# The first two modulation vectors of a diffusion trunk step: three pairs of split buffers, and the token norm and turns spread over both vectors

## Chip, cores and metric

The kernel runs on one core of a Trainium2 chip, as one launch. The metric is the time of an execution on the device in microseconds (us). A profile covers one execution.

## What is computed

The reference is one inference step of a one-layer trunk: 512 latent and 128 context tokens, 2048 channels. The part around the change is the first modulation and norm, which the value projection needs (`c` for the latent, `c_ctx` for the context tokens):

```python
m = silu(cvec) @ w_mod + b_mod                 # (2048) @ (2048 x 12288), for c and for c_ctx
sh1, sc1, g1, sh2, sc2, g2 = split(m, 6)
h = rmsnorm(x, g_pre1) * (1 + sc1) + sh1       # 640 tokens x 2048
proj = h @ w_in                                # value columns are made first
```

Then come a bidirectional recurrence and differential attention, their projections, and a mixture of 16 experts. All weights are float32.

## The kernel before

**Splitting.** Every float32 weight is cut into a high and a low part for TensorE: ScalarE copies the tile in `raw` (four slots of 128 x 2048, 1 MiB each) into `w_hi` (L339), VectorE subtracts it from the tile into `w_lo` (L348). `w_hi` and `w_lo` have two slots each (NHL). SP loads a tile as two DMAs of 512 KB (`load`, L432 to L436) once the low part of the tile four earlier is made. ScalarE makes a high part only when TensorE is done with the tile two earlier (`halves_used`). With `fine=True` all this goes by halves of 1024 columns.

**First two vectors.** Shift and scale (sh1, sc1) are columns 0 to 4095 of w_mod, 16 tiles of 128 x 2048 for each vector, group g = 0 and g = 1, taken in the order of the k rows. TensorE multiplies each tile by a 128 x 4 stationary `c_hl` (silu(c) and silu(c_ctx), high and low), eight matmuls of 512 columns a tile (L385, L386, in `by_halves`). Group 0 accumulates in banks 4 to 7 of PSUM, group 1 in banks 0 to 3. At a group's end VectorE and ScalarE each copy half of the row (`mod_half`, L1165 and L808), TensorE turns it into columns (`turn_rows`), and VectorE adds the bias and makes the scale (`mod_columns`, L1149 to L1154).

**Tokens.** ScalarE's queue issues the five token blocks of 1 MiB (128 tokens x 2048) behind tiles 5, 7, 9, 11 and 13 of group 0. In group 1, every third tile, ScalarE squares a block (`square`, L775, with its root, L777), VectorE makes a diagonal of the reciprocals (`norm_diagonal`, L1133, L1135), TensorE turns and scales the block by 16 matmuls against that diagonal into banks 4 to 7 (`turn_x`, L1739), and ScalarE and VectorE take two banks each into `xT` (`take_x`, L783 and L1140). Once the second row is in columns, `tokens(k)` makes h in its high part (ScalarE) and its low part (VectorE, L1159), and the value projection starts (`wide`, matmuls on L419 to L421): two halves of 512 columns, each of four tiles of w_in. The five blocks of a half are copied into `v_stage` by VectorE (`take_values`, L1194).

**Small loads and POOL.** ScalarE's queue first issues c, c_ctx, the gain g_pre1, the bias and the identity; TensorE waits for all five (80) and turns the 80 rows (L1727), VectorE copies the columns (L1124), ScalarE applies Silu (L763). In program order ScalarE makes the high part of tile 0 before that. POOL issues 11 parameter loads (L588), sets `zero` and writes it over the 5 MiB accumulator `d_f` of the experts in five DMAs (L594) that wait for nothing else. Then, for each value half, it stores `v_stage` (L600, L602) and waits for the store, which frees `v_stage`. The parameters are turned by TensorE behind everything else of this stage.

**Order.** Each engine's order is written out by hand; the engines meet only at semaphores. The rest of the kernel (input projection with modulation vectors 2 to 5 made on VectorE, heads, output, experts) is untouched.

Of the kernel before, what the change touches and what calls it, by code (L numbers as in the profile page):

```python
# [22 lines left out]
P = 128  # L23
# [34 lines left out]
N_PAR = 11  # L58
# [5 lines left out]
MOD_FROM = [sum(MOD_TILES[:n]) for n in range(8)]  # L64

# [37 lines left out]
def trunk(nc, a, out_ctx, out_lat, out_k, out_v, out_state):  # L103
    ctx = ExitStack()
    with ctx:
# [42 lines left out]
        def place(at0, items):  # L148

            o, made = at0, {}  # L150
            for name, shape, dt in items:
# [10 lines left out]
                       ("zero", [P, D], F32), ("rows1", [80, P], F32), ("rows2", [105, P], F32),  # L162
                       ("cols1", [P, 80], F32), ("cols2", [P, 105], F32),
# [4 lines left out]
        A["diag"] = at("diag", [P, 2, P], F32, s0 + 50048 + 256)  # L168
        c_hl = at("c_hl", [P, KT, 4], F32R, s0 + 50048)
# [7 lines left out]
        assert s0 + 15360 + 2 * UB <= PLACED["rows1"] and PLACED["ones2"] + 64 <= s0 + 50048  # L177
# [90 lines left out]
        par_loaded, x_lat_loaded, x_ctx_loaded = sem("par_loaded"), sem("x_lat_loaded"), sem("x_ctx_loaded")  # L268
# [34 lines left out]
        LATER = {"state_turned": ("rows_turned", 2), "state_row": ("cols_ready", 2), "state_stored": ("c_loaded", 80),  # L303
# [75 lines left out]
        def by_halves(pe, u, slot, out, c, start, stop):  # L379

            for p in range(2):
                pe.wait_ge(lo_ready, 2 * NRAW + 2 * u + p + 1)
                for n in (2 * p, 2 * p + 1):
                    s = slice(n * 512, (n + 1) * 512)
                    pe.matmul(out[:, n, :], c, w_lo[:, slot, s], start=start, stop=False)  # L385
                    last = pe.matmul(out[:, n, :], c, w_hi[:, slot, s], start=False, stop=stop)  # L386
                last.then_inc(halves_used, 1)
# [170 lines left out]
        def _(pool):  # L558
# [14 lines left out]
            def heads(x):  # L573
# [10 lines left out]
                     (r2[104:105, :], a["g_sub"])]  # L584
            loads += [(A["lamv"][0:1, i, :], a[n]) for i, n in enumerate(("lam_q1", "lam_q2", "lam_k1", "lam_k2"))]
# [165 lines left out]
        def _(act):  # L751
# [11 lines left out]
            act.activation(A["sc"][:], A["cols1"][:, 0:32], ACT.Silu).then_inc(S["c_act"], 1)  # L763
# [31 lines left out]
            for k in range(KT):  # L795
                split_hi(act, Q_MOD, k + 1, fine=True)
                if k >= 4 and k % 2 == 0 and (k - 4) // 2 < TT:
                    t = (k - 4) // 2
                    if t < TT - 1:
                        act.dma_start(x_in[:, t, :], a["x_sample"][0][t * P:(t + 1) * P, :]).then_inc(x_lat_loaded, 16)  # L800
                    else:
                        act.dma_start(x_in[:, t, :], a["x_prompt"][0]).then_inc(x_ctx_loaded, 16)

            def mod_half(g):

                act.wait_ge(halves_used, used((Q_MOD + g * 4 + 4) * 4))
                b = 6 - 4 * g
                act.activation(A[f"m_row{g}"][:, 1024:2048].rearrange("p (b n) -> p b n", b=2), ps[0:4, b:b + 2, :], ACT.Copy  # L808
                               ).then_inc(S["row_act"], 1)

            for k in range(KT):
                split_hi(act, Q_MOD + 4, k + 1, fine=True)
                if k == 0:
                    mod_half(0)
                if k % 3 == 0 and k < 3 * TT:
                    square(k // 3)
                if k % 3 == 0 and k:
                    take_x(k // 3 - 1)
# [290 lines left out]
        def _(dve):  # L1109
# [14 lines left out]
            dve.tensor_copy(A["cols1"][:], ps[:, 7, 0:80]).then_inc(S["cols_ready"], 1)  # L1124
# [3 lines left out]
            split_lo(dve, Q_MOD, 0)  # L1128
# [14 lines left out]
            def mod_columns(g, h):  # L1143
# [5 lines left out]
                own.done(TTn(dst, r[:, 0:2, :], A["cols1"][:, None, 48 + n:56 + n].to_broadcast([P, 2, 8]), ALU.add))  # L1149
                own.settle()  # L1150
                own.done(TTn(dst, r[:, 2:4, :], dst, ALU.add))
                if g:
                    own.settle()
                    STT(A["A1"][:, :, 8 * h:8 * h + 8], dst, 1.0, A["cols1"][:, None, 32 + 8 * h:40 + 8 * h].to_broadcast([P, 2, 8]),  # L1154
# [6 lines left out]
            def mod_half(g):  # L1161

                dve.wait_ge(halves_used, used((Q_MOD + g * 4 + 4) * 4) - 1)
                b = 4 - 4 * g
                dve.tensor_copy(A[f"m_row{g}"][:, 0:1024].rearrange("p (b n) -> p b n", b=2), ps[0:4, b:b + 2, :]  # L1165
                                ).then_inc(S["m_row_ready"], 1)

            for k in range(KT):
                split_lo(dve, Q_MOD, k + 1, fine=True)
            for k in range(KT):  # L1170
                split_lo(dve, Q_MOD + 4, k + 1, fine=True)
                if k == 0:
                    mod_half(0)
                if k == 1:
                    mod_columns(0, 0)
                    mod_columns(0, 1)
                if k % 3 == 1 and k < 3 * TT:
                    norm_diagonal(k // 3)
                if k % 3 == 0 and k:
                    take_x(k // 3 - 1)  # L1180
# [19 lines left out]
            dve.wait_ge(S["rows_turned"], 2)  # L1200
            dve.tensor_copy(A["cols2"][:], ps[:, 5, 0:105]).then_inc(S["cols_ready"], 1)

            dve.wait_ge(S["cols_ready"], 2)
# [519 lines left out]
        def _(pe):  # L1723
# [5 lines left out]
            pe.wait_ge(S["c_loaded"], 80)  # L1729
            turn(ps[:, 7, 0:80], A["rows1"][:], 80).then_inc(S["rows_turned"], 1)  # L1730
# [12 lines left out]
            def mod_group(g, after=()):  # L1743

                b = 4 - 4 * g
                for k in range(KT):
                    by_halves(pe, Q_MOD * NRAW + g * KT + k, k % 2, ps[0:4, b:b + 4, :], c_hl[:, k, :], k == 0, k == KT - 1)
                    if k in after:
                        after[k]()

            def turn_rows(g):

                if g:
                    pe.wait_ge(S["xt_act"], 2 * TT)
# [9 lines left out]
            def turn_parameters():  # L1764
                pe.wait_ge(par_loaded, N_PAR * 16)
                pe.wait_ge(S["xt_dve"], 2 * TT)
# [8 lines left out]
            mod_group(0)  # L1775
            turns = {3 * t + 2: (lambda t=t: turn_x(t)) for t in range(TT)}
# [344 lines left out]
```

## Time and profile before

| | us |
|---|---|
| median of 3 runs (lowest, highest) | 3057.34 (3056.35, 3059.58) |
| the profiled execution's own time | 3056.34 |
| its span, from first to last instruction | 3054.8 |
| TensorE matmuls busy | 2882.4 (94%) |
| VectorE, ScalarE, GpSimd (POOL) busy | 2141.5, 1544.1, 289.8 |

The mean granted TensorE clock is 0.973 of full speed (2.4 GHz). All places on the time axis count from the span's start. "Busy" of TensorE takes in overlapping, pipelined matmuls. A chain of waits is followed back from the last instruction: at each step to what released it. A table of windows gives each engine's busy time in a stretch, the granted clock (PEclk), the mean busy share of the 16 DMA engines and their GB/s. In timelines and groups, x and a number counts instructions, and the bracket says what the engine waited for.

### The profile page before, as it was taken

Reading aid. Unit: us, or ns where it says so; the run is one execution under the profiler, and the core shown is the slowest. Engines: PE = TensorE matmul, PEld = TensorE weight load, DVE = VectorE, ACT = ScalarE, POOL = GpSimd, SP = SyncE. Lnnn points to the kernel's source line nnn. Section 1 sums busy time; section 2 is a strip of 40 time slices with the busy share of each in tenths; the row PEclk is TensorE's granted clock in tenths of the full one; section 3 lists DMA queues with packets and bytes.
Section 4 is the critical chain, followed back from the end, with each engine's and each line's share of the span. In section 5 each row is a group of like instructions: output and inputs, shape, how many; then the busy total and the mean of one; then the engine's idle time right before and its main releaser. Section 6 shows DMA issues by size and latency. Waiting matters only on the chain.

```text
span 3054.8 us, 42269 instructions
## 1 busy us (share of the span) xinstructions
PE 2882.4 (94%) x15607; PEld 2304.1 (75%) x15607; DVE 2141.5 (70%) x1836; ACT 1544.1 (51%) x1469; POOL 289.8 (9%) x349
## 2 busy tenths in 40 slices
PE   5899999999999999989999995999999999999993
PEld 1589999998788888879997774666666666666662
DVE  4737797795566666653344457888888888888886
ACT  4931212213455555542233343777777777777773
POOL 1000000002111111100000000011000000111100
PEclk8999999999999999999999997999999999999997
DMA  9737686683333333344433564899999999999995
GB/s 387 275 92 261 206 273 220 207 286 114 116 115 115 115 115 115 115 150 126 121 111 137 196 231 174 347 372 389 379 389 378 395 386 382 387 379 381 381 393 218
DMA packets 292998, 758.17 MB, mean 248 GB/s; under 512 B 20328, under 2 KB 184736, under 8 KB 228144
## 3 DMA queue, kind: packets, MB, share of 16 engines
q1 hardware_dynamic: 266768, 638.80, 57.5%
q0 software_dynamic: 23680, 102.59, 10.3%
q10 hardware_dynamic: 2480, 15.84, 1.3%
q8 instruction: 44, 0.72, 0.1%
q14 instruction: 26, 0.21, 0.0%
HBM read 700.94 MB, written 56.22 MB: 248 GB/s over the span
## 4 chain that ended last, share of the span: by engine, by line
PE 81%; DVE 9%; DMA 5%; issue 3%; ACT 2%; DVEq 0%; POOL 0%; SPq 0%; POOLq 0%; ACTq 0%
PE ps L419 15%; PE ps L420 14%; PE ps L421 14%; PE ps L1814 8%; PE ps L1816 7%; PE ps L1815 7%; DVE mod_acc L1261 4%; PE ps L1948 2%; PE ps L1950 2%; PE ps L1949 2%; PE ps L1727 2%; DMA raw<-in_w_mod 2%; DVE w_lo L348 1%; PE ps L1877 1%; PE ps L1899 1%
## 5 line engine op out<-in xcount | busy, mean ns | idle before, releaser
L373 DVE TENSOR_TENSOR we_lo<-raw,we_hi 128x2048 fp32r<-128x2048 f32 x384 | 876.4, 2290 | 138.9 <-ACT we_hi L368 137.9
L368 ACT ACTIVATE we_hi<-raw 128x2048 fp32r<-128x2048 f32 x384 | 736.5, 1919 | 287.6 <-PE ps L421 287.6
L1814 PE MATMUL ps<-hi,w_lo 128*128 128x320 f32 x2048 | 647.2, 316 | 9.4 <-DVE w_lo L348 5.1
L1816 PE MATMUL ps<-hi,w_hi 128*128 128x320 f32 x2048 | 634.2, 310 | 0.0
L1815 PE MATMUL ps<-lo,w_hi 128*128 128x320 f32 x2048 | 634.0, 310 | 0.0
L348 DVE TENSOR_TENSOR w_lo<-raw,w_hi 128x2048 fp32r<-128x2048 f32 (+1 forms) x184 | 349.8, 1918 | 254.9 <-ACT w_hi L339 248.7
L339 ACT ACTIVATE w_hi<-raw 128x2048 fp32r<-128x2048 f32 (+1 forms) x184 | 292.5, 1610 | 281.5 <-PE ps L421 156.2
L1814 PEld LDWEIGHTS ps<-hi,w_lo 128*128 128x128 f32 x2048 | 385.8, 188 | 28.2 <-issue 14.9
L419 PE MATMUL ps<-we_hi,xs_lo 128*80 128x512 f32 x1024 | 402.2, 393 | 2.2 <-DVE xs_lo L1658 2.2
L420 PE MATMUL ps<-we_lo,xs_hi 128*80 128x512 f32 x1024 | 402.7, 393 | 0.0
L421 PE MATMUL ps<-we_hi,xs_hi 128*80 128x512 f32 x1024 | 400.1, 391 | 0.0
L1815 PEld LDWEIGHTS ps<-lo,w_hi 128*128 128x128 f32 x2048 | 385.9, 188 | 1.4
L1816 PEld LDWEIGHTS ps<-hi,w_hi 128*128 128x128 f32 x2048 | 385.5, 188 | 0.0
L1261 DVE SCALAR_TENSOR_TENSOR mod_acc<-mod_raw,sc,mod_acc 128x2048 f32<-128x2048 f32 x120 | 276.7, 2347 | 3.6
L419 PEld LDWEIGHTS ps<-we_hi,xs_lo 128*80 128x80 f32 x1024 | 151.6, 148 | 87.2 <-issue 2.8
L421 PEld LDWEIGHTS ps<-we_hi,xs_hi 128*80 128x80 f32 x1024 | 151.6, 148 | 84.2 <-issue 0.5
L420 PEld LDWEIGHTS ps<-we_lo,xs_hi 128*80 128x80 f32 x1024 | 151.7, 148 | 82.3 <-issue 0.4
L419 PE MATMUL ps<-we_hi,hid_lo 128*80 128x512 f32 x512 | 202.3, 395 | 0.5 <-DVE hid_lo L1678 0.4
L421 PE MATMUL ps<-we_hi,hid_hi 128*80 128x512 f32 x512 | 200.7, 392 | 0.0
L420 PE MATMUL ps<-we_lo,hid_hi 128*80 128x512 f32 x512 | 200.5, 392 | 0.0
L1948 PE MATMUL ps<-hi,w_lo 128*128 128x320 f32 x512 | 160.9, 314 | 14.7 <-DVE lo L1448 9.6
L1949 PE MATMUL ps<-lo,w_hi 128*128 128x320 f32 x512 | 159.6, 312 | 0.0
(339 smaller groups left out, 3704.5 us busy)
## 6 DMA issues: line engine op xcount, KB each, us to landing
raw<-in_w_e_gate SPq DMA_DIRECT2D x128, 1024.0 KB, 7.2
raw<-in_w_e_up SPq DMA_DIRECT2D x128, 1024.0 KB, 6.9
raw<-in_w_e_down SPq DMA_DIRECT2D x128, 1024.0 KB, 12.0
raw<-in_w_in SPq DMA_DIRECT2D x144, 512.0 KB, 5.1
mod_raw<-in_w_mod SPq DMA_DIRECT2D x64, 1024.0 KB, 5.1
raw<-in_w_mod SPq DMA_DIRECT2D x64, 512.0 KB, 7.7
raw<-in_w_o SPq DMA_DIRECT2D x64, 512.0 KB, 4.7
d_proj<-stage POOLq DMA_DIRECT2D x32, 320.0 KB, 3.3
```

The lines of the kernel that those rows point to most:

```text
L339: act.activation(w_hi[:, j % NHL, s], raw[:, j, s], ACT.Copy).then_inc(hi_ready, 1 if fine else 2)
L348: dve.tensor_tensor(w_lo[:, j % NHL, s], raw[:, j, s], w_hi[:, j % NHL, s].bitcast(F32), ALU.subtract).then_inc(lo_ready, 1 if fine else 2)
L368: act.activation(we_hi[:, k % NEH, :], raw_slot(k), ACT.Copy).then_inc(hi_ready, 2)
L373: TTn(we_lo[:, k % NEH, :], raw_slot(k), we_hi[:, k % NEH, :].bitcast(F32), ALU.subtract).then_inc(lo_ready, 2)
L419: pe.matmul(out, s_lo, m_hi, start=start, stop=False)
L420: pe.matmul(out, s_hi, m_lo, start=False, stop=False)
L421: return pe.matmul(out, s_hi, m_hi, start=False, stop=stop)
L1261: last = STT(mod_acc[:, v, :], w, c, mod_acc[:, v, :], ALU.mult, ALU.add)
L1814: pe.matmul(out, wl, hi[:, k, ms], start=(k % 16 == 0), stop=False)
L1815: pe.matmul(out, wh, lo[:, k, ms], start=False, stop=False)
L1816: last = pe.matmul(out, wh, hi[:, k, ms], start=False, stop=(k == KT - 1))
L1948: pe.matmul(out, wl, hi[:, k, ms], start=(k % 8 == 0), stop=False)
```

## The change

A third pair of buffers, `w3_hi` and `w3_lo`, is laid over space that `mod_raw` takes later; tile m of the 32 (both groups in one count) uses pair m mod 3, so ScalarE waits for TensorE to be done with the tile three earlier. Both groups accumulate in banks 0 to 3, and tile 16 waits until the first row has been copied out. Token loads, squares, turns and takes are spread over all 32 tiles. The gain g_pre1 and the bias leave ScalarE's first loads for POOL's parameter loads (`rows3`), and are turned, with the other parameters, behind tile 3 of TensorE. Silu is applied once to a constant ahead of the data. Tile 0's high part now stands behind c's on ScalarE. POOL writes the zeros only after the first value half, ahead of its store. `cols1` shrinks to c and c_ctx, and the values of LATER go with it.

```diff
-N_PAR = 11
+N_PAR = 13
+X_LOAD = (1, 4, 8, 13, 17)
+X_SQUARE = (6, 11, 16, 22, 26)
+X_DIAG = (7, 12, 17, 23, 27)
+X_TAKE = (10, 15, 20, 26, 30)
...
+        w3_hi, w3_lo = at("w3_hi", [P, D], F32R, mod_at), at("w3_lo", [P, D], F32R, mod_at + UB)
+        c_hl = at("c_hl", [P, KT, 4], F32R, mod_at + 2 * UB)
+        A["diag"] = at("diag", [P, 2, P], F32, mod_at + 2 * UB + 256)
...
+        def mod_w(m):
+            return ((w_hi[:, 0, :], w_lo[:, 0, :]), (w_hi[:, 1, :], w_lo[:, 1, :]), (w3_hi[:], w3_lo[:]))[m % 3]
+        def tile_hi(act, m):
+            act.wait_ge(raw_loaded[m % NRAW], (m // NRAW + 1) * INC)
+            for p in range(2):
+                if 2 * m + p > 1:
+                    act.wait_ge(halves_used, 2 * m + p - 1)
+                act.activation(mod_w(m)[0][:, half_of(p)], raw[:, m % NRAW, half_of(p)], ACT.Copy).then_inc(hi_ready, 1)
+        def tile_lo(dve, m):
+            for p in range(2):
+                dve.wait_ge(hi_ready, 2 * m + p + 1)
+                dve.tensor_tensor(mod_w(m)[1][:, half_of(p)], raw[:, m % NRAW, half_of(p)],
+                                  mod_w(m)[0][:, half_of(p)].bitcast(F32), ALU.subtract).then_inc(lo_ready, 1)
...
@@ gpsimd
+            loads += [(A["rows3"][0:16, :], flat(a["g_pre1"][0])), (A["rows3"][16:48, :], flat(a["b_mod"][0, 0:2 * D]))]
...
-            for t in range(TT):
-                pool.dma_start(d_f[t * P:(t + 1) * P, :], A["zero"][:]).then_inc(S["zero_stored"], 16)
-            with pool.Fori(0, 2) as c:
+            for c in range(2):
                 wait(pool, "bank_taken", TT * (c + 1))
-                plain()
+                if c == 0:
+                    for t in range(TT):
+                        pool.dma_start(d_f[t * P:(t + 1) * P, :], A["zero"][:]).then_inc(S["zero_stored"], 16)
                 pool.dma_start(d_v[:, bass.ds(c * 512, 512)].rearrange("(t p) n -> p t n", p=P), v_stage[:]
...
@@ scalar
-            for dst, src in ((r1[0:16, :], a["c"][0]), (r1[16:32, :], a["c_ctx"]), (r1[32:48, :], a["g_pre1"][0]),
-                             (r1[48:80, :], a["b_mod"][0, 0:2 * D])):
+            for dst, src in ((r1[0:16, :], a["c"][0]), (r1[16:32, :], a["c_ctx"])):
...
-            split_hi(act, Q_MOD, 0)
+            act.wait_ge(S["const_set"], 1)
+            act.activation(misc[:, 4:5], eps_col, ACT.Silu)
...
+            tile_hi(act, 0)
             def square(t):
-                if t == 0:
-                    act.wait_ge(x_lat_loaded, (TT - 1) * 16)
-                    act.wait_ge(S["const_set"], 1)
-                if t == TT - 1:
-                    act.wait_ge(x_ctx_loaded, 16)
+                act.wait_ge(x_loaded[t % 2], (t // 2 + 1) * 16)
...
+            for m in range(1, 2 * KT + 1):
+                if m < 2 * KT:
+                    tile_hi(act, m)
+                else:
+                    split_hi(act, Q_V, 0, fine=True)
+                if m in X_LOAD:
+                    t = X_LOAD.index(m)
+                    src = a["x_sample"][0][t * P:(t + 1) * P, :] if t < TT - 1 else a["x_prompt"][0]
+                    act.dma_start(x_in[:, t, :], src).then_inc(x_loaded[t % 2], 16)
+                if m == KT:
                     mod_half(0)
+                if m in X_SQUARE:
+                    square(X_SQUARE.index(m))
+                if m in X_TAKE:
+                    take_x(X_TAKE.index(m))
...
@@ vector
+            for m in range(1, 2 * KT + 1):
+                if m < 2 * KT:
+                    tile_lo(dve, m)
+                else:
+                    split_lo(dve, Q_V, 0, fine=True)
+                if m == 6:
+                    dve.wait_ge(S["rows_turned"], 2)
+                    own.done(dve.tensor_copy(A["cols_b"][:], ps[:, 4, 0:48]))
+                    own.done(dve.tensor_copy(A["cols2"][:], ps[:, 5, 0:105]))
+                    own.settle()
+                if m == KT:
                     mod_half(0)
+                if m == X_DIAG[3]:
                     mod_columns(0, 0)
                     mod_columns(0, 1)
+                if m in X_DIAG:
+                    norm_diagonal(X_DIAG.index(m))
+                if m in X_TAKE:
+                    take_x(X_TAKE.index(m))
...
@@ tensor
-            pe.wait_ge(S["c_loaded"], 80)
-            turn(ps[:, 7, 0:80], A["rows1"][:], 80).then_inc(S["rows_turned"], 1)
+            pe.wait_ge(S["c_loaded"], 48)
+            turn(ps[:, 7, 0:32], A["rows1"][:], 32).then_inc(S["rows_turned"], 1)
...
+            def mod_tile(m):
+                w = mod_w(m)
+                for p in range(2):
+                    pe.wait_ge(lo_ready, 2 * NRAW + 2 * m + p + 1)
+                    if m == KT and p == 0:
+                        wait(pe, "m_row_ready", 1)
+                    if m == KT and p == 1:
+                        pe.wait_ge(S["row_act"], 1)
+                    for n in (2 * p, 2 * p + 1):
+                        s = slice(n * 512, (n + 1) * 512)
+                        pe.matmul(ps[0:4, n, :], c_hl[:, m % KT, :], w[1][:, s], start=(m % KT == 0), stop=False)
+                        last = pe.matmul(ps[0:4, n, :], c_hl[:, m % KT, :], w[0][:, s], start=False, stop=(m % KT == KT - 1))
+                    last.then_inc(halves_used, 1)
...
-                if g:
-                    pe.wait_ge(S["xt_act"], 2 * TT)
+                pe.wait_ge(S["xt_act"], (6, 2 * TT)[g])
...
+            for m in range(2 * KT):
+                mod_tile(m)
+                if m == 3:
+                    turn_parameters()
+                if m in X_DIAG:
+                    turn_x(X_DIAG.index(m))
+                if m == X_TAKE[2]:
+                    turn_rows(0)
             turn_rows(1)
-            turn_parameters()
```

`turn_parameters` no longer waits for `xt_dve`; it turns `rows3` into bank 4 and `rows2` into bank 5.

## Rows read from the trace of the kernel before

**Rows 1.** The page's first line: the span of the profiled execution.

```profile
span 3054.8 us, 42269 instructions
```

**Rows 2.** Chain of waits, 0 to 330 us: start us, us, what.

```profile
53.39 12.92 DMA raw<-in_w_mod
...
88.24 0.43 PE ps L386
...
100.55 3.57 PE ps L1739 x32
...
109.74 3.57 PE ps L1739 x32
...
138.60 0.76 PE ps L419
```

**Rows 3.** Timelines of VectorE and POOL; an issue from the DMA view, 180 to 260.

```profile
247.51 3.34 DVE L1194 COPY v_stage<-ps 128x512 f32<-128x512 f32 x5 [6.49 <-PE ps L421]
...
196.67 0.89 POOL L600 DMA_DIRECT2D d_v<-v_stage  x1 [180.39 <-DVE v_stage L1194]
...
d_v<-v_stage POOLq DMA_DIRECT2D x2, 1280.0 KB, 6.2
```

**Rows 4.** Table of windows; columns: window, us, engines' busy, PEclk, DMA share, GB/s.

```profile
0.00:20.00 20.00, 5.12 (x13) 1.62 (x14) 6.75 (x13) 8.95 (x9) 10.29 (x21) 1.00 0.87 316
40.00:60.00 20.00, 11.17 (x43) 2.83 (x42) 11.38 (x11) 10.07 (x11) 0.00 (x0) 1.00 1.02 414
100.00:120.00 20.00, 20.00 (x127) 12.66 (x126) 18.54 (x22) 19.53 (x24) 0.00 (x0) 1.00 0.92 327
```

**Rows 5.** DMA view: traffic in 30 to 50 us; issues in 0 to 140.

```profile
DMA packets 1909, 8.23 MB, mean 412 GB/s; under 512 B 221, under 2 KB 221, under 8 KB 1587
...
raw<-in_w_mod SPq DMA_DIRECT2D x64, 512.0 KB, 7.7
d_f<-zero POOLq DMA_DIRECT2D x5, 1024.0 KB, 10.5
...
x_in<-in_x_sample ACTq DMA_DIRECT2D x4, 1024.0 KB, 8.0
```

**Rows 6.** Timelines of ScalarE, VectorE, TensorE and POOL, 0 to 30 us.

```profile
3.03 0.45 ACTq L759 DMA_DIRECT2D ident<-in_ident  x1
7.69 1.28 ACT L339 ACT_TABLE_LOAD   x1 [7.69 <-DMA raw<-in_w_mod]
...
10.43 0.24 DVE L1124 COPY cols<-ps 128x80 f32<-128x80 f32 x1 [8.10 <-PE ps L1727]
...
10.00 0.39 PE L1727 MATMUL ps<-ident,rows 80*128 80x80 f32 x1 [10.00 <-DMA ident<-in_ident]
...
6.66 0.96 POOL L588 DMA_DIRECT2D lamv<-in_lam_k  x2
...
13.62 2.66 POOL L594 DMA_DIRECT2D d_f<-zero  x5 [4.18 <-issue]
```

**Rows 7.** Timelines of ScalarE and VectorE, 78 to 140 us.

```profile
92.23 1.90 ACT L775 ACTIVATE junk<-x_in 128x2048 f32<-128x2048 f32 x1
...
94.45 1.06 ACT L783 ACTIVATE xT<-ps 128x512 f32<-128x512 f32 x2
...
105.15 5.80 ACT L339 ACTIVATE w_hi<-raw 128x1024 fp32r<-128x1024 f32 x6 [0.21 <-PE ps L386]
...
108.52 0.16 DVE L1133 RECIPROCAL stats<-stats 128x1 f32<-128x1 f32 x1
...
108.91 4.63 DVE L348 TENSOR_TENSOR w_lo<-raw,w_hi 128x1024 fp32r<-128x1024 f32 x4
113.45 1.28 DVE L1140 COPY xT<-ps 128x512 f32<-128x512 f32 x2
...
133.04 1.20 DVE L1165 COPY m_row<-ps 4x1024 f32<-4x1024 f32 x1
```

**Rows 8.** Table of windows of 2 us, columns as in rows 4.

```profile
70.00:72.00 2.00, 2.00 (x6) 0.56 (x5) 2.00 (x2) 0.90 (x1) 0.00 (x0) 0.50 1.01 412
```

More of the change, by code:

```diff
@@ L176, in trunk @@
         m_row2 = at("m_row2", [2, D], F32, s0)
-        assert s0 + 15360 + 2 * UB <= PLACED["rows1"] and PLACED["ones2"] + 64 <= s0 + 50048
+        assert s0 + 15360 + 2 * UB <= PLACED["rows1"] and mod_at + NMOD * UB <= s_end
         v_stage = at("v_stage", [P, TT, 512], F32, s0)
@@ L300, in trunk @@
             "stage_free", "g_stage_free", "k_new_free", "o_n_free", "ye_free")}
-        LATER = {"state_turned": ("rows_turned", 2), "state_row": ("cols_ready", 2), "state_stored": ("c_loaded", 80),
+        LATER = {"state_turned": ("rows_turned", 2), "state_row": ("cols_ready", 1), "state_stored": ("c_loaded", 48),
                  "rrows_turned": ("rows3_turned", 4), "bias_in": ("lam_val", 1), "bias_out": ("lam_spread", 1),
@@ L793, in tokens @@
                 act.activation(hi[:, k, :], xT[:, k, :], ACT.Copy).then_inc(S["tok_hi"], 1)
[L795 to L802, printed above, removed]
             def mod_half(g):
                 act.wait_ge(halves_used, used((Q_MOD + g * 4 + 4) * 4))
-                b = 6 - 4 * g
-                act.activation(A[f"m_row{g}"][:, 1024:2048].rearrange("p (b n) -> p b n", b=2), ps[0:4, b:b + 2, :], ACT.Copy
+                act.activation(A[f"m_row{g}"][:, 1024:2048].rearrange("p (b n) -> p b n", b=2), ps[0:4, 2:4, :], ACT.Copy
                                ).then_inc(S["row_act"], 1)
-            for k in range(KT):
-                split_hi(act, Q_MOD + 4, k + 1, fine=True)
-                if k == 0:
+            for m in range(1, 2 * KT + 1):
[8 more added lines that the diff above has]
+                if m == KT:
                     mod_half(0)
[L815 to L818, printed above, removed]
+                if m in X_SQUARE:
+                    square(X_SQUARE.index(m))
+                if m in X_TAKE:
+                    take_x(X_TAKE.index(m))
             mod_half(1)
@@ L1127, in _ @@
                 ).then_inc(S["c_ready"], 1)
-            split_lo(dve, Q_MOD, 0)
+            tile_lo(dve, 0)
             def norm_diagonal(t):
@@ L1148, in mod_columns @@
                 dst = A["cols3"][:].rearrange("p (v n) -> p v n", v=2)[:, :, n:n + 8]
-                own.done(TTn(dst, r[:, 0:2, :], A["cols1"][:, None, 48 + n:56 + n].to_broadcast([P, 2, 8]), ALU.add))
+                own.done(TTn(dst, r[:, 0:2, :], A["cols_b"][:, None, 16 + n:24 + n].to_broadcast([P, 2, 8]), ALU.add))
                 own.settle()
@@ L1163, in mod_half @@
                 dve.wait_ge(halves_used, used((Q_MOD + g * 4 + 4) * 4) - 1)
-                b = 4 - 4 * g
-                dve.tensor_copy(A[f"m_row{g}"][:, 0:1024].rearrange("p (b n) -> p b n", b=2), ps[0:4, b:b + 2, :]
+                dve.tensor_copy(A[f"m_row{g}"][:, 0:1024].rearrange("p (b n) -> p b n", b=2), ps[0:4, 0:2, :]
                                 ).then_inc(S["m_row_ready"], 1)
[L1168 to L1172, printed above, removed]
+            for m in range(1, 2 * KT + 1):
[9 more added lines that the diff above has]
+                if m == KT:
                     mod_half(0)
-                if k == 1:
+                if m == X_DIAG[3]:
                     mod_columns(0, 0)
                     mod_columns(0, 1)
[L1177 to L1180, printed above, removed]
+                if m in X_DIAG:
+                    norm_diagonal(X_DIAG.index(m))
+                if m in X_TAKE:
+                    take_x(X_TAKE.index(m))
             mod_half(1)
@@ L1741, in turn_x @@
                     last.then_inc(S["x_turned"], 1)
[L1743 to L1749, printed above, removed]
+            def mod_tile(m):
[11 more added lines that the diff above has]
+                    last.then_inc(halves_used, 1)
             def turn_rows(g):
-                if g:
-                    pe.wait_ge(S["xt_act"], 2 * TT)
+                pe.wait_ge(S["xt_act"], (6, 2 * TT)[g])
                 for h in range(2):
@@ L1765, in turn_parameters @@
                 pe.wait_ge(par_loaded, N_PAR * 16)
-                pe.wait_ge(S["xt_dve"], 2 * TT)
+                turn(ps[:, 4, 0:48], A["rows3"][:], 48)
                 turn(ps[:, 5, 0:105], A["rows2"][:], 105).then_inc(S["rows_turned"], 1)
@@ L1774, in _ @@
             pe.wait_ge(S["c_ready"], 1)
-            mod_group(0)
-            turns = {3 * t + 2: (lambda t=t: turn_x(t)) for t in range(TT)}
-            turns[1] = lambda: turn_rows(0)
-            mod_group(1, turns)
+            for m in range(2 * KT):
[6 more added lines that the diff above has]
+                    turn_rows(0)
             turn_rows(1)
-            turn_parameters()
             leave(pe)
```

24 lines of the change are left out of this document (6 added, 18 removed).

## The prediction

> **What bounds the kernel now.** The profiled execution has a span of 3054.8 us [rows 1] and a time of 3056.34 us, 1.0 below the median of 3057.34 of the three runs; sums are made against 3056.34 and 1.0 is added at the end. I looked first at where the changed code runs: everything it touches lies ahead of the first matmul of the value projection, at 138.60 us [rows 2]. From then on the chain runs through TensorE, and at the end of the first value half VectorE waits 6.49 us for TensorE, not the reverse [rows 3]. So the question is how much earlier than 138.60 the value projection can start, and whether what follows keeps that.
>
> The table of windows [rows 4] shows two regimes. Up to 80 us the DMA engines are full (share 1.02 at 414 GB/s in 40 to 60 us), while VectorE works 11.38 and ScalarE 10.07 of 20 us: the modulation tiles arrive late, because 5 MiB of zeros [rows 5] (zeros written from the start) and 5 MiB of tokens travel among them; the chain shows one such wait of 12.92 us [rows 2]. From 80 us on it is reversed: TensorE is busy 20.00 of 20 us and DMA has fallen to 0.92. The chain there has a period of 109.74 - 100.55 = 9.19 us for three tiles and one token turn of 3.57 us [rows 2], so a tile costs TensorE (9.19 - 3.57) / 3 = 1.87 us. Token norm and turns are heaped on the second vector, when transfer has slack, and absent in the first, when compute has.
>
> **The change, part by part.** The useful floor is four sums, one per resource, for the stretch up to the value projection.
>
> DMA. 64 issues of 512 KB for w_mod plus five token blocks of 1 MiB are 37 MiB, 38.8 MB; the zeros' five issues of 1 MiB go away from here [rows 5]. The first four tiles are in flight from the start, as now; in the old run about 4.4 MB are over by 14.7 us (316 GB/s over the first 20 us [rows 4], of which the zeros, issued from 13.62 [rows 6], are the rest). The other 33 MiB, 34.6 MB, at the 412 GB/s measured in 30 to 50 us [rows 5] take 84 us: the last w_mod tile lands at 14.7 + 84.2 = 98.9 us.
>
> Start. Three loads instead of five stand ahead of the first turn; the identity is issued at 3.03 and the turn runs at 10.00 [rows 6]. Two issues of 0.45 us less: about 9.2. The Silu table load moves ahead of the data; the one at 7.69 (1.28 [rows 6]) and its like before Silu leave the path, but ScalarE now makes tile 0 after c, not before. cols at 9.7, silu and copy 0.5, high half 1.0, low half 1.2: TensorE starts at 12.5, and tile 0 is free for a reload at 13.6, when the DMA engines are just about done with the first batch. So the start costs DMA nothing and is worth nothing by itself.
>
> ScalarE. Six high halves take 5.80 us, 1.93 a tile; a square with its root 94.45 - 92.23 = 2.22; a take 1.06 [rows 7]. From 10.2 us: 33 tiles 63.8, five squares 11.1 and one root table 1.28, five takes 5.3, the row copy 1.0, five x issues at the identity's 0.45, 2.3: it could end at 95.0.
>
> VectorE. Four low halves 4.63, so 2.31 a tile; a take 1.28; reciprocal and diagonal 108.91 - 108.52 = 0.39 [rows 7]. From 11.2 us: 33 tiles 76.4, five takes 6.4, diagonals 2.0, one row copy 1.2, the small columns 1.1 (the two parameter copies of 0.24 among them, each the size of the copy at 10.43 [rows 6]): 98.3 if it never waits. TensorE: from 12.5, 32 tiles 59.8, five turns 17.9, first tiles at half clock 2, parameter turns and first row turns 2, and a new wait at tile 16, where both vectors now share banks 0 to 3: VectorE makes tile 16's second half and the row copy first, 2.4. That is 96.6, and ahead of the last tile it is hidden.
>
> So all four lie between 95 and 99, with 15 us of transfer per five tiles and a block (6 x 2.55) against 13 us of work on each engine. DMA ends last, and what counts is the tail. **Floor:** tile 31 lands 98.9, two high halves to 100.8, low 102.2, V tile 0 low 104.5; from the row copy's start at 133.04 to 138.60 the old run takes 5.56 us [rows 2, 7], unchanged: value projection at 110.1. **Taken:** the last heap does not fit. At tile 26 ScalarE has a square and a take, 3.3 us, with 5 tiles left. Tile 26 lands at 98.9 - 5 x 2.55 = 86.1; two halves 88.1, square and take 91.4, half of 27 at 92.4; then VectorE, slower per tile (2.31) than ScalarE, has five tiles, a diagonal, a take and V tile 0: 11.6 + 0.4 + 1.3 + 2.3 = 15.6, to 108.0, and 5.56: 113.5. Saved 138.6 - 113.5 = 25.1 us. The earlier heaps (tiles 16, 22) are met in the same way, and recovered at about 0.25 to 0.6 us a tile; what is not recovered is the upper side of the range.
>
> Moved zeros. Their five issues and the d_v store stand behind each other on POOL's queue after the first value half (now 196.67 [rows 3], then about 171.6): 2.66 us of issue [rows 6] and 5.24 MB / 412 = 12.7 us ahead of the store that frees v_stage, against a landing 6.2 us after issue so far [rows 3]. It would land near 193; VectorE needs it for the second half at 247.51 - 25 = 222 [rows 3]. Cover 29 us, cost nothing; without cover, 13 to 20 us. The parameter loads grow from 11 to 13 on POOL and are wanted after tile 3, near 21 us, when the last, issued near 9 (two take 0.96 and ended at 7.62 [rows 6]), is long there: nothing. The POOL loop unrolled, the semaphores, LATER: nothing.
>
> The page "DMA: Bandwidth & Descriptors" of the Trainium skill (Specifications) gives an HBM limit per core of about 358 GB/s; by it the 34.6 MB would need 97 us, not 84, and the start move to 126. The row of 412 GB/s speaks against it for one running core.
>
> **Rivals.** (1) TensorE or the mutual waits bind (0.17): three buffers are six halves, and turns, takes and diagonals wait for each other across engines. For it: TensorE was full in the old second regime, and has only 2 us of slack per five tiles. Each tile at half clock costs 8 matmuls x (0.43 [rows 2] - 1.87 / 8) = 1.6 us; five to eight such tiles, or heaps unrecovered, give a start of 118 to 130: 3036.7 to 3048.7. (2) Slower than before (0.02): TensorE's clock stays low. The granted clock was 0.50, the 1.2 GHz level, even while it was busy 2.00 of 2 us (70 to 72 us [rows 8]). If all 32 tiles ran at 0.43 a matmul, TensorE would need 12.5 + 110 + 18 + 5 = 145.5 and the value projection start near 151: 3069.7. It decides once more than four tiles run so, and turns to a loss beyond some 22. Against it: in 100 to 120 us, with shorter gaps, the clock is 1.00 [rows 4]. "TensorE: Matmul & The Clock Gate" of the Trainium skill (HAM oscillation) says that waits for DMA between tiles throttle the engine again each time; by that rule this rival would hold, and the trace agrees only where the gaps are of several us, which here go away. (3) The gain is given back (0.05): the zeros collide with the w_in and modulation loads of the second value half, or v_stage comes late: up to 12.7 us back, 3045. (4) The buffers absorb all heaps and the start lies at 107 to 110 (0.04): 3025.5 to 3029.
>
> **Numbers.** The forecast case, a start of 110 to 118 (3028.7 to 3036.7), has 0.72. The likeliest: 3056.34 - 25.1 + 1.0 = 3032.2. The range for 8 in 10 takes that case and the near edges of (1) and (4): 3027 to 3040. A measurement can tell about 0.2%, 6 us, from no change: faster by more has 0.96, since (1), (3) and (4) are faster too; same 0.02 (a mild form of the second rival); slower 0.02.
>
> **What would show it.** Right: the first value matmul at 110 to 118; DMA at or near 1.0 and 410 GB/s from 15 to 95 us; no issue to d_f before the value projection; in the chain no transfer wait above a few us; TensorE clock near 1.0 from 40 to 95; value projection as long as before and v_stage free in time. Wrong: DMA below 0.9 in the middle, with ScalarE waiting for TensorE (rival 1); half clock with TensorE full (rival 2); VectorE waiting for the release of v_stage, or high halves for w_in, after 170 us (rival 3).

## The result, and the profile after

The changed kernel took 3038.36 us in the median of six runs (3034.41 to 3043.57), the kernel before, beside it, 3057.76 (3051.86 to 3059.59): a ratio of 0.9938, 95% interval 0.9926 to 0.9949. It is 19.4 us faster, where 25.1 were forecast, and inside the range of 3027 to 3040. The profiled execution took 3038.86 us. Its page:

```profile
span 3037.3 us, 42260 instructions
...
PE 2880.1 (95%) x15608; PEld 2306.8 (76%) x15608; DVE 2140.8 (70%) x1838; ACT 1542.2 (51%) x1470; POOL 288.6 (10%) x351
```

Busy times have hardly moved; only idle time at the beginning went. The table of windows of the changed kernel, columns as in [rows 4]:

```profile
0.00:20.00 20.00, 8.25 (x25) 2.34 (x25) 8.06 (x14) 8.72 (x11) 8.58 (x18) 1.00 0.86 326
20.00:40.00 20.00, 13.72 (x42) 4.00 (x43) 13.74 (x16) 15.82 (x18) 0.00 (x0) 0.78 1.03 411
40.00:60.00 20.00, 19.82 (x116) 12.03 (x115) 17.34 (x18) 15.63 (x19) 0.00 (x0) 0.96 0.99 380
60.00:80.00 20.00, 17.10 (x80) 8.06 (x79) 16.98 (x20) 15.85 (x20) 0.00 (x0) 0.83 1.02 397
80.00:100.00 20.00, 19.11 (x109) 9.38 (x107) 17.96 (x23) 19.29 (x23) 0.00 (x0) 1.00 0.95 336
100.00:120.00 20.00, 14.15 (x87) 8.40 (x87) 16.06 (x23) 13.98 (x19) 0.00 (x0) 0.92 0.98 363
```

The two regimes of [rows 4] are gone: from 20 us on every engine works 14 to 20 of 20 us. But the last column, which the sum held at 412 GB/s, falls to 380 and then to 336. The chain of waits of the changed kernel shows what that leads to (start, us, what):

```profile
53.81 7.73 DMA raw<-in_w_mod
...
73.37 7.85 DMA raw<-in_w_mod
...
102.91 0.39 SPq L452
103.48 6.71 DMA raw<-in_w_in
110.22 1.07 ACT w_hi L346
111.31 2.36 DVE w_lo L355 x2
113.67 1.13 DVE m_row L1173
...
119.15 0.76 PE ps L435
```

At the place of the 12.92 of [rows 2] the chain now has 7.73. In all, its waits for transfers of w_mod are 36.2 us in four pieces (9.59, 11.07, 7.73, 7.85), where the chain before had 53.6 us in five (5.33, 15.99, 10.72, 12.92, 8.63). The first value matmul, at 138.60 before, is at 119.15, not at 113.5. The tail is instructive: the load of value tile 0 is issued only at 102.91, when the low part of tile 28 is made, because there are four raw slots; it lands 6.7 us later, and high part, low part, row copy and columns follow it in line.

Behind that point nothing is given back that could be laid to the change. The zeros now lie behind the first value half (timeline of POOL, changed kernel):

```profile
176.87 2.65 POOL L614 DMA_DIRECT2D d_f<-zero  x5 [166.48 <-DVE v_stage L1208]
179.51 0.89 POOL L615 DMA_DIRECT2D d_v<-v_stage  x1
...
231.83 0.87 POOL L615 DMA_DIRECT2D d_v<-v_stage  x1 [50.88 <-DVE v_stage L1208]
```

and VectorE's timeline has the second half taken:

```profile
228.19 3.34 DVE L1208 COPY v_stage<-ps 128x512 f32<-128x512 f32 x5 [6.49 <-PE ps L437]
```

VectorE takes the second half at 228.19 after waiting for TensorE, the same 6.49 us as before [rows 3], not for the release of `v_stage`. The slowest store of `v_stage` took 17.7 us to land; the last of them was issued at 180.4, so it was free by about 198, 30 us ahead.

### The profile page after: what moved, and what is told of

It is laid out like the page before. It is cut to its first block, busy times and chain, and to the rows that moved or that the text cites. A ratio compares the mean times of both kernels' runs of the same rounds, so it can differ in the third digit from the quotient of the medians.

```text
span 3037.3 us, 42260 instructions
## 1 busy us (share of the span) xinstructions
PE 2880.1 (95%) x15608; PEld 2306.8 (76%) x15608; DVE 2140.8 (70%) x1838; ACT 1542.2 (51%) x1470; POOL 288.6 (10%) x351
## 4 chain that ended last, share of the span: by engine, by line
PE 80%; DVE 9%; DMA 4%; issue 4%; ACT 2%; SPq 0%; DVEq 0%; POOL 0%; ACTq 0%; POOLq 0%
PE ps L435 15%; PE ps L436 14%; PE ps L437 14%; PE ps L1833 8%; PE ps L1835 7%; PE ps L1834 7%; DVE mod_acc L1271 4%; PE ps L1967 2%; PE ps L1968 2%; PE ps L1969 2%; PE ps L1737 2%; PE ps L1896 1%; PE ps L1918 1%; DMA raw<-in_w_mod 1%; PE ps L1880 1%
## 5 line engine op out<-in xcount | busy, mean ns | idle before, releaser
L355 DVE TENSOR_TENSOR w_lo<-raw,w_hi 128x2048 fp32r<-128x2048 f32 (+1 forms) x121 | 274.9, 2273 | 221.3 <-ACT w_hi L346 215.1
L346 ACT ACTIVATE w_hi<-raw 128x2048 fp32r<-128x2048 f32 (+1 forms) x121 | 229.2, 1896 | 246.2 <-PE ps L437 156.5
```

The costliest lines, as they stand in the source:

```text
L346: act.activation(w_hi[:, j % NHL, s], raw[:, j, s], ACT.Copy).then_inc(hi_ready, 1 if fine else 2)
L355: dve.tensor_tensor(w_lo[:, j % NHL, s], raw[:, j, s], w_hi[:, j % NHL, s].bitcast(F32), ALU.subtract).then_inc(lo_ready, 1 if fine else 2)
```

## The experiments

Two measures are used. The time of a kernel scatters by some 9 to 12 us between executions of the same kernel. In the profiles the first value matmul is steadier, and what comes behind it (the run's time less that moment) lay between 2915.4 and 2925.0 us over the fourteen profiles, 2917.7 before and 2919.7 after, with no order by what was changed. The profiles also show where 1.9 of the 2 us lie that are missing between the 19.45 won at the first value matmul and the 17.5 of the spans. The stretch from the router's last matmul on its fourth block of tokens to the first expert matmul is 36.5 us long in the profile before and 38.4 in the one after. In it the router's matmuls of the fifth block took 5.29 us before, at a mean granted clock of 0.68, and 6.99 after, at 0.50, the 1.2 GHz level. The change does not touch these matmuls. TensorE was busy throughout in both, and the clock fell in the course of them before, and ahead of them after. Why it fell at that moment, no run here tells. The mean granted clock of whole executions of the changed kernel also differs, 0.978 in one of 3034.53 us and 0.973 in one of 3043.57.

### Two pairs of buffers, zeros early, work heaped

Three parts of the change were undone, one at a time.

```diff
@@ e1_two_pairs
-            return (...)[m % 3]
+            return (...)[m % 2]
-                if 2 * m + p > 1:
-                    act.wait_ge(halves_used, 2 * m + p - 1)
+                act.wait_ge(halves_used, 2 * m + p + 1)
```

> The changed kernel with two pairs of split buffers in place of three; all else as changed. In the changed kernel the first value matmul is at 119.15 us. Theory A (the reload of the four raw slots is what thins the transfers, and the third pair covers TensorE's turns): each of the five turns of 3.6 us now holds ScalarE back, the start moves to 122 to 128 and the time rises by 3 to 9 us. Rival (transfers bind anyway, ScalarE waited only 0.8 us for TensorE): under 1.5 us.

Measured: first value matmul at 128.61, a little beyond the 122 to 128 expected; 3046.66 us in the median of 8, ratio to before 0.9969 (0.9959 to 0.9980). The third pair is worth 8 us of time. The waits of that profile name the mechanism (waits, 0 to 129 us: who waited for whom, us, times, longest):

```profile
ACT w_hi L395 <- PE ps L1764: 21.2, 11, 4.3
```

In the changed kernel ScalarE waits 0.8 us in all for TensorE in this stretch. A turn of 3.6 us on TensorE now stops ScalarE, its high parts stop the low parts, and they the reloads: the rate from 20 to 100 us is 366 GB/s. The chain of this kernel runs through TensorE behind tile 16 too, where its matmuls take 0.43 us in place of 0.23 from 69.79 to 74.48, so a part of the 8 us is the price of the clock and not of the turns.

```diff
@@ e2_zeros_early (and nothing behind the first value half)
             leave(pool)
+            for t in range(TT):
+                pool.dma_start(d_f[t * P:(t + 1) * P, :], A["zero"][:]).then_inc(S["zero_stored"], 16)
```

> The changed kernel with the five stores of zeros back at the beginning, ahead of everything that POOL waits for. If transfer is the scarce thing in this stretch, 5.24 MB at the 380 to 411 GB/s seen there cost 12.8 to 13.8 us: first value matmul at 132 to 133, time up by 13. If the engines' heaps bind, transfers have slack and it costs under 6 us.

Measured: 130.34, and 3051.14 us in the median of 10, ratio 0.9982 (0.9972 to 0.9991). It is 11.2 us at the first value matmul, where 12.8 to 13.8 were expected, and 12.8 in the time: the bytes cost very nearly what their transfer takes, and this is the largest part by either median, though at the first value matmul by less than the 2 us by which that moment scatters (9.5 for the third pair). In its chain one wait for a raw tile lasts 23.21 us, from 17.42. Four slots moved 423 GB/s from 20 to 40 us here, with zeros and tokens queued beside the tiles, and 383 from 80 to 100.

```diff
@@ e3_heaped
-X_LOAD = (1, 4, 8, 13, 17)
-X_SQUARE = (6, 11, 16, 22, 26)
-X_DIAG = (7, 12, 17, 23, 27)
-X_TAKE = (10, 15, 20, 26, 30)
+X_LOAD = (5, 7, 9, 11, 13)
+X_SQUARE = (17, 20, 23, 26, 29)
+X_DIAG = (18, 21, 24, 27, 30)
+X_TAKE = (20, 23, 26, 29, 32)
...
-                act.wait_ge(x_loaded[t % 2], (t // 2 + 1) * 16)
+                act.wait_ge(x_loaded[t % 2], (3, 2)[t % 2] * 16)
```

> The changed kernel with the token loads behind tiles 5 to 13 and all squares, diagonals, turns and takes in the second vector, every third tile, as before the change; three pairs and late zeros stay. If TensorE's 9.19 us per three tiles and a turn come back as the bound of the second vector, the first value matmul moves to 124 to 130, the time up by 5 to 11 us. If spreading was worth nothing beside the moved zeros, it stays within 2 us of 119.15.

Measured: 123.89, at the edge of the 124 to 130 expected; 3046.15 us in the median of 5, ratio 0.9964 (0.9949 to 0.9978). The chain of this kernel shows the old period again:

```profile
76.12 3.57 PE ps L1749 x32
...
85.25 3.57 PE ps L1749 x32
...
94.38 3.57 PE ps L1749 x32
```

9.13 us for three tiles and a turn, as in [rows 2], though there is a third pair: there TensorE's sum of work was the bound, not the buffers. The spread won 4.7 to 6.7 us at the first value matmul. Undone singly, the parts cost 8, 13 and 8 us of time against 3038.36, 29 in sum and so more than the 19.4 of all together: what one part wins depends on the others being there. (Taken from the ratios to the kernel before they are 9.5, 13.5 and 8, each within some 4 us.)

### How many raw slots

The open question was why the transfers fell below 412 GB/s.

```diff
@@ e4_six_slots
+        def m_raw(m):
+            j = (m + 4) % 6
+            return raw[:, j, :] if j < NRAW else (A["m_spare"][:], raw_x[0][:])[j - NRAW]
...
+            for m in range(2 * KT):
+                if m >= 6:
+                    sp.wait_ge(lo_ready, 2 * NRAW + 2 * (m - 5))
...
+                    sp.dma_start(m_raw(m)[:, half_of(p)], ...).then_inc(raw_loaded[(m + 4) % 6], INC // 2)
...
+            for kq in range(4):
+                sp.wait_ge(lo_ready, 2 * NRAW + 2 * (2 * KT - 6 + kq + 1))
...
```

`m_spare` takes the place of the second row, which moves onto the first; the sixth slot lies where `zero` was, which POOL now sets after the first value half.

> The changed kernel with six slots of raw tiles in this stretch in place of four (two lie where the second row and the zeros were; the zeros are set later). Theory A (a late low part delays the reload, so the transfers run thin, 336 GB/s from 80 to 100 us): mean rate from 20 to 100 us rises to 395 or more, first value matmul at 110 to 115, time down by 4 to 9 us. Rival B (this stream of 4 KB rows doesn't move faster than some 380 GB/s, whatever is outstanding): rate as before, within 1.5 us. Rival C (ScalarE and VectorE bind): within 2 us, with their waits for raw tiles near 0.

Measured: first value matmul at 114.06; median of four 3037.75 us, ratio 0.9947 (0.9930 to 0.9963), which the scatter of the rest does not tell from the changed kernel's: the 4 to 9 us expected of the time did not show. Table of windows:

```profile
20.00:40.00 20.00, 14.63 (x62) 5.28 (x61) 14.05 (x17) 15.18 (x16) 0.00 (x0) 0.91 1.03 415
40.00:60.00 20.00, 18.89 (x107) 10.00 (x106) 17.75 (x19) 16.74 (x21) 0.00 (x0) 1.00 1.02 408
60.00:80.00 20.00, 17.22 (x96) 8.84 (x95) 18.34 (x21) 18.05 (x21) 0.00 (x0) 0.91 1.03 411
80.00:100.00 20.00, 20.00 (x119) 11.59 (x118) 18.92 (x25) 19.61 (x25) 0.00 (x0) 1.00 1.03 407
```

The same transfers, in the same rows of 4 KB, hold 407 to 415 GB/s to the end. So this shape of stream is not capped at 380 GB/s; with four slots too little is outstanding. (The edit also writes SP's loops over the two vectors and over the value halves out; no run has that with four slots.) ScalarE still waits 9.7 us for raw tiles from 20 to 100 us, in place of 15.4, so rival C, with waits near 0, fell too.

The changed kernel was run again as a control, and the two rivals were tried by themselves:

> The changed kernel, unaltered, as a control beside the others of this chip. If the profiles can be compared to a us, the first value matmul lies within 1 us of 119.15 and the last w_mod tile's high part begins within 1 us of 107.59; the rest of the span scatters by some 7 us between executions (2917.7 to 2925.0 us from the first value matmul to the end's time in the six profiles so far).

Measured: first value matmul at 117.2, last tile's high part at 105.41, 3040.14 us in the median of four, ratio 0.9950 (0.9933 to 0.9967). The control missed the 1 us that was expected: with four slots the moment scatters by 2 us, and its rate from 20 to 100 us was 391 GB/s against 381. Differences are read against both profiles from here on.

```diff
@@ e6_one_transfer
-                         [(raw[:, k % NRAW, half_of(p)], w_mod[k * P:(k + 1) * P, bass.ds(g * D + p * 1024, 1024)])
-                          for p in range(2)])
+                         [(raw[:, k % NRAW, :], w_mod[k * P:(k + 1) * P, bass.ds(g * D, 2048)])], INC)
```

> The changed kernel with each modulation tile loaded by one DMA of 1 MiB in rows of 8 KB in place of two of 512 KB in rows of 4 KB; four slots. Theory A (depth of outstanding loads): nothing changes in the rate, first value matmul within 1.5 us of 119.15. Rival B (the shape of the transfers limits the rate): the rate from 40 to 100 us rises from 371 to above 395 and the start comes 4 to 8 us earlier.

Measured: 115.2, 395 GB/s from 20 to 100 us, 3039.02 us (ratio 0.9950, 0.9933 to 0.9966). From 40 to 100 us, the stretch that the expectation names, it moved 386 GB/s, where the two profiles of the changed kernel have 371 and 384: the 395 of rival B did not come. The start lies 2 to 4 us earlier than in those profiles, between the two expectations. Whether the shape matters a little with four slots is not shown, as the moment scatters by 2 us; it does not bring the 410 GB/s of more slots.

```diff
@@ e7_short_squares
-                own.done(act.activation(A["junk0"][:], x_in[:, t, :], ACT.Square, accum_out=stats[:, t:t + 1]))
+                own.done(act.activation(A["junk0"][:, 0:64], x_in[:, t, 0:64], ACT.Square, accum_out=stats[:, t:t + 1]))
```

> The changed kernel with each square over 64 of the 2048 columns of its token block (the rest of the sum of squares is left out), four slots: 1.7 us less of ScalarE at each of five places, 8.4 us in all, and no work less for VectorE, TensorE or DMA. Theory A (ScalarE's heaps delay low parts and so the reloads): first value matmul 3 to 7 us earlier, rate from 80 to 100 us above 360. Rival (VectorE alone, or the transfers alone, set the pace): under 1.5 us.

Measured: 115.8, 398 GB/s, 3037.71 us (ratio 0.9944, 0.9927 to 0.9960); 368 GB/s from 80 to 100 us. Taking 8.4 us of work from ScalarE brings 1.5 to 3.4 us: the direction of theory A, at the lower edge of its size or under it. The mark of 360 GB/s from 80 to 100 us tells nothing, since the control has 377 there with the squares whole. That the squares are one cause of late low parts agrees with this but is not shown by it; they are not the only one.

```diff
@@ e10_five_slots (against e4_six_slots; zero is set at the start again)
-            j = (m + 4) % 6
+            j = (m + 3) % 5
...
```

> Five slots of raw tiles instead of four or six, all else as changed. Theory A (depth of outstanding loads) gives a value between: mean rate from 20 to 100 us between 392 and 410 GB/s, first value matmul at 114.5 to 117. If it is a threshold that only six pass, the values of four slots stay (381 to 392, 117 to 119).

Measured, one execution: first value matmul at 113.98, 410 GB/s from 20 to 100 us, 3032.90 us. The moment is no value between, just ahead of the 114.5 to 117 expected: the fifth slot brings all that the sixth did. The zeros are set at the start here, so where they are set was not what counted. Over all profiles with everything else as changed, the rates of 20 to 100 us are

| raw slots | GB/s, 20 to 100 us | first value matmul, us |
|---|---|---|
| 4 (two profiles) | 381, 391 | 119.15, 117.2 |
| 5 | 410 | 113.98 |
| 6 | 410 | 114.06 |

### The start

```diff
@@ e9_start_undone
+            tile_hi(act, 0)
-            act.wait_ge(S["const_set"], 1)
-            act.activation(misc[:, 4:5], eps_col, ACT.Silu)
             act.wait_ge(S["cols_ready"], 1)
...
-            tile_hi(act, 0)
```

> The changed kernel with tile 0's high part again ahead of Silu on ScalarE and no early table load; the three first loads, four slots and all else as changed. The prediction costs the start at nothing: high part and two table loads again stand before c, TensorE's first tile begins about 3 us later than in the changed kernel, and the first value matmul stays between 117 and 119.5, where the two profiles of the changed kernel had it. Rival: the start is on the path through the transfers (tile 4 can be loaded only when tile 0's low part is made), and the first value matmul comes 2 to 4 us later.

Measured, one execution: TensorE's first tile at 12.46 in place of 10.05, first value matmul at 117.7, between the two of the control. Timelines of TensorE, first of the changed kernel:

```profile
6.10 0.31 PE L1737 MATMUL ps<-ident,rows 32*128 32x32 f32 x1 [6.10 <-DMA ident<-in_ident]
10.05 0.59 PE L1764 MATMUL ps<-w_lo,c_hl 128*4 128x512 f32 x1 [3.64 <-DVE w_lo L402]
```

and of the kernel with the start undone:

```profile
5.67 0.31 PE L1737 MATMUL ps<-ident,rows 32*128 32x32 f32 x1 [5.67 <-DMA ident<-in_ident]
12.46 0.58 PE L1764 MATMUL ps<-w_lo,c_hl 128*4 128x512 f32 x1 [6.48 <-DVE w_lo L402]
```

The 2.4 us at the start are worth nothing that a first value matmul known to 2 us can show.

### The order of the tail

```diff
@@ e8_six_row_first (six slots; VectorE, m = 32)
-                else:
-                    split_lo(dve, Q_V, 0, fine=True)
...
             mod_columns(1, 1)
+            split_lo(dve, Q_V, 0, fine=True)
```

> Six raw slots, and on VectorE the copy of the second row and its columns ahead of the low part of value tile 0. With six slots the first value matmul was at 114.06, and VectorE worked without a gap from 84 us to the row copy at 108.49. If that order is on the path, the row copy starts 2.3 us earlier, near 106.2, and the first value matmul lies at 111.5 to 112.5, provided TensorE is done with tile 31's first half by then; if value tile 0 binds instead, 113 to 114.

Measured: row copy at 107.01, first value matmul at 113.6, so the expectation of 111.5 to 112.5 fell; 3035.08 us, ratio 0.9936 (0.9920 to 0.9953). Two waits took the place of the one removed: the row copy waits 0.58 us for TensorE, still late from the turn behind tile 27, and the 2.35 us of value tile 0 now stand ahead of the first token's low part. Hence the next two, with all token work earlier and the low part of value tile 0 in two halves (`value_low`) that fill the gaps:

```diff
@@ e11_tuned_four, e12_tuned_six
+X_LOAD = (1, 3, 6, 10, 15)
+X_SQUARE = (5, 9, 14, 19, 23)
+X_DIAG = (6, 10, 15, 20, 24)
+X_TAKE = (9, 13, 18, 23, 27)
...
-                else:
-                    split_lo(dve, Q_V, 0, fine=True)
-                if m == 6:
+                if m == 5:
...
             mod_half(1)
+            value_low(0)
             mod_columns(1, 0)
             mod_columns(1, 1)
+            value_low(1)
```

> Four slots; token loads, squares, turns and takes some tiles earlier (last turn behind tile 24, last take at 27), and on VectorE the second row's copy ahead of the low part of value tile 0, whose two halves fill its waits. If the heap at tile 26 is what costs the tail, the first value matmul comes 3 to 5 us earlier, at 113 to 115; theory A says that the heaps only move and the transfers still run thin (rate of 20 to 100 us under 398), so only the 2.3 us of order are won: 115 to 117.

Measured with four slots: 114.1, 391 GB/s, 3038.70 us (ratio 0.9941, 0.9924 to 0.9957). That is 3.1 us earlier than the control and 5.1 than the first profile. The order was put at 2.3, and with a moment that scatters by 2 us the difference alone does not show that the heap counted. VectorE's timeline in the control does:

```profile
96.32 2.36 DVE L402 TENSOR_TENSOR w_lo<-raw,w_hi 128x1024 fp32r<-128x1024 f32 x2 [1.40 <-ACT w_hi L396]
98.60 0.16 DVE L1142 RECIPROCAL stats<-stats 128x1 f32<-128x1 f32 x1
...
99.00 6.90 DVE L402 TENSOR_TENSOR w_lo<-raw,w_hi 128x1024 fp32r<-128x1024 f32 x6
105.81 1.28 DVE L1149 COPY xT<-ps 128x512 f32<-128x512 f32 x2
...
111.55 1.21 DVE L1173 COPY m_row<-ps 4x1024 f32<-4x1024 f32 x1
```

It waits 1.40 us for a high part that stands behind the square and the take of tile 26 on ScalarE, and then has no gap up to the row copy: the heap was on the path there, as the prediction had it. The rate of e11_tuned_four is the control's 391, thin as theory A had it.

> The same order and six slots. Six slots had the first value matmul at 114.06, with the row copy first at 113.63, where it waited for TensorE (0.58 us) and then for the low part of value tile 0. With the last turn at tile 24 TensorE is out of the way: row copy at 105.5 to 106.5, first value matmul at 111 to 112.5, rate from 20 to 100 us 407 to 411, the best of all; median at 3032 to 3036. Rival (VectorE's sum of work alone decides): no earlier than 113.

Measured with six: row copy at 105.65, first value matmul at 111.5, 410 GB/s; 3033.57 us in the median of four (3027.21 to 3036.09), ratio 0.9926 (0.9909 to 0.9942). VectorE then has no gap at the tail (its timeline in that kernel):

```profile
96.44 4.62 DVE L409 TENSOR_TENSOR w_lo<-raw,w_hi 128x1024 fp32r<-128x1024 f32 x4
100.98 2.35 DVE L409 TENSOR_TENSOR w_lo<-m_spare,w_hi 128x1024 fp32r<-128x1024 f32 x2
103.25 2.35 DVE L409 TENSOR_TENSOR w_lo<-raw_x,w_hi 128x1024 fp32r<-128x1024 f32 x2
105.65 1.21 DVE L1184 COPY m_row<-ps 4x1024 f32<-4x1024 f32 x1
```

It has the best median of the versions run four times or more, and beats the kernel before clearly; against the changed kernel, whose interval overlaps its own, the 5.8 to 7.7 us of its first value matmul are the firmer evidence.

## Why the prediction was right, and where its sum was off

**The range.** The time lies in the range, but beyond the forecast case: that case ended at a start of 118 and 3036.7 us, and the profile has 119.15 (the control 117.2) and the median 3038.36. It is inside because the range took in the near edge of rival (1). Of the signs of being right, three failed: DMA moved 380 and 336 GB/s where 410 were to hold, the chain has transfer waits of 7.7 to 11.1 us, and the granted clock from 60 to 80 us is 0.83.

**The bound before.** Right. Zeros back early cost 12.8 us; work heaped again brought back TensorE's 9.13 us per three tiles and a turn.

**DMA, the term that was mis-sized.** "The other 33 MiB, 34.6 MB, at the 412 GB/s measured in 30 to 50 us take 84 us: the last w_mod tile lands at 98.9 us." In the changed kernel its high part began at 107.59, 8.7 us later, at 381 GB/s in the mean of 20 to 100 us. The error was to carry a rate over from a stretch in which a token block was nearly always queued beside the four tiles (issued at 34.39, 42.00 and 49.27, some 8 us each to landing; the zeros had landed by 34), to one in which the blocks come 11 to 16 us apart and then end, and the tiles' slots are released late. The rates of the changed kernel follow this: 397 GB/s from 60 to 80 us, with the last block issued at 66.51, and 336 from 80 to 100, with the tiles alone. [rows 4] already had 327 GB/s for tiles alone, put down there to TensorE. With five or six slots the 410 GB/s are there, and the last tile's high part begins at 101.39 with six, 0.60 of it a wait for TensorE, not for its load. So the mechanism was right, and the term was mis-sized by the depth of the loads that it rests on.

**The tail.** From the last tile's landing to the first value matmul the sum had 14.6 us, of which 3.4 were the heap at tile 26; the changed kernel took 119.15 - 107.59 = 11.56, near the floor's 11.2. With the load so late, ScalarE had caught up and the heap was hidden in this profile. In the control it was not: there VectorE worked from 96.32, behind the heap, to the row copy at 111.55, 15.2 us where the sum had 15.6, and 5.7 to the first value matmul, where it had 5.56. The whole sum of the tail held, from a start 3.9 us later than its 92.4. With six slots the tail took 12.7 us, and moving the heap and the order of the tail won 2.6 us there and 3.1 to 5.1 with four slots. In the changed kernel, 8.7 late at the load less 3.0 won back in the tail gives the 5.65 us by which the first value matmul was missed. The forecast of 113.5 is what five or six slots measure, 114.0.

**The start.** Worth nothing, as costed, though its times were off: the first turn ran at 6.10, not 9.2, and TensorE began at 10.05, not 12.5.

**The wait at tile 16.** Forecast 2.4 us, hidden. The wait was 2.90 us, and it had a price that the sum did not have, in the clock. Windows of 2 us of the changed kernel:

```profile
64.00:66.00 2.00, 0.00 (x0) 0.00 (x0) 2.00 (x2) 2.00 (x2) 0.00 (x0) 0.86 1.02 406
66.00:68.00 2.00, 1.72 (x5) 0.54 (x6) 0.47 (x2) 1.97 (x5) 0.00 (x0) 0.50 1.05 395
68.00:70.00 2.00, 2.00 (x6) 0.58 (x5) 2.00 (x3) 2.00 (x3) 0.00 (x0) 0.50 1.03 358
70.00:72.00 2.00, 2.00 (x6) 0.62 (x5) 1.97 (x5) 2.00 (x3) 0.00 (x0) 0.50 0.99 403
72.00:74.00 2.00, 2.00 (x15) 1.59 (x14) 2.00 (x3) 0.37 (x1) 0.00 (x0) 0.93 0.96 371
```

TensorE does nothing from 64 to 66 us and then runs at the 1.2 GHz level for more than 6 us, though busy. In this profile TensorE is not in the chain there, from 45.5 us to the turn of the second row, so it cost nothing; with two pairs of buffers the same stretch is in the chain. No run took this wait away.

**The rivals.** (1), mutual waits, holds in part: they act through the raw slots, and the start of 119.15 lies at the near edge of its 118 to 130. Its sign was another, ScalarE waiting for TensorE with DMA below 0.9: it waited 0.8 us, and DMA was at 0.95 or above. (2), a clock that stays low, did not come: 1.00 from 80 to 100 us. "TensorE: Matmul & The Clock Gate" of the Trainium skill (HAM oscillation) has waits for DMA throttle the engine again; the trace agrees for 20 to 40 us (0.78), where TensorE's waits lead back to transfers, and not for the gap of 0.86 us ahead of 87.73, with 1.00 after it. The fall at tile 16 follows a wait for a copy, not for a transfer. (3), the gain given back behind the zeros, did not: the wait of VectorE for the second half is the same 6.49 us. The prediction places this wait at the end of the first value half; the row, at 247.51, is that of the second, and at the first VectorE waited 1.14 us. TensorE is what it waits for in both, so nothing changes. The 358 GB/s per core that "DMA: Bandwidth & Descriptors" of the Trainium skill (Specifications) gives as the HBM limit is not what the slower 381 was: one core alone moved 410 over 80 us.

## What to carry over

A transfer rate read in one stretch holds in another only if as much is outstanding there: ask what releases the slots, and how late the slowest of these releases comes. When work is spread so that all engines near their sums, count the slots of the loads again: here a fifth slot brought the first value matmul forward by 3.2 to 5.2 us, as much as a better order did with four (3.1 to 5.1), and both together 5.8 to 7.7; the medians of the times do not tell these apart. And undo parts one at a time: here they cost 8, 13 and 8 us singly, for 19 together.

## What the runs showed of the hardware

With four slots of 1 MiB the DMA engines showed a busy share of 0.99 and 1.01 from 20 to 100 us and moved 381 and 391 GB/s; with five, 1.03 and 410. A share near 1.0 did not mean that the rate was at its height.

The 64 KB identity load, issued at 2.09 us on ScalarE's queue in the changed kernel, was there at 6.10; in the other seven profiles with four slots and loads of 512 KB it was there at 5.64 to 5.75, with one load of 1 MiB for each tile at 7.00. With five slots the turn that waits for it ran at 8.90, with six at 8.57 to 9.20: more or earlier big loads on SP's queue delayed a small one on another queue by 2.5 to 3.6 us. Why it was earlier than before the change (10.00 [rows 6]), by more than its earlier issue, was not tried.
